# Streaming-encoder block: waits per half, spare banks in the mixer, one u tile ahead of the last scores, and index steps of four heads for the dense blocks

## The reference, cut to what matters

```python
hn = rmsnorm(x, mix_norm_w)                       # x: 512 tokens x 1024
z, xbc, dt, q, k, v = split(hn @ w_in)
y_ssd  = rmsnorm_per_group(ssd(silu(conv(xbc)), dt) * silu(z))    # Mamba-2, 8 heads, chunks of 64, state carried on
y_diff = rmsnorm_per_head(softmax(q1 k1) v - lam * softmax(q2 k2) v)   # 4 heads, chunk-causal
x = x + concat(y_ssd, y_diff) @ w_out
xb = rmsnorm(x, ffn_norm_w)                       # PEER, for every token:
sc = (xb @ w_q) . sub_keys                        # 8 heads x 2 halves x 128 keys
s, i = top_k(sc, 16)                              # per half
top_s, pos = top_k(s[0] + s[1], 16)               # of 16 x 16 candidates
idx = (i[0] * 128 + i[1])[pos];  g = softmax(top_s)
h = gelu(u[idx] @ xb)                             # u, v: 16384 x 1024
out = x + sum((g * h) * v[idx])                   # 128 experts for each token
```

## Time and profile before

| what | value |
|---|---|
| median of three runs | 1458.4 us (1455.88 to 1465.24) |
| the profiled execution | 1465.86 us, span 1464.1 us |
| TensorE busy | 1384.9 us, 95% of the span |
| VectorE busy | 1124.6 us, 77% |
| ScalarE busy | 392.5 us, 27% |
| GpSimd busy | 621.6 us, 42% |
| moved | 466.65 MB, mean 319 GB/s |

### The profile page before, as it was taken

The page is one execution under the profiler, slowest core; times in us unless marked ns, Lnnn a source line. Parts: engine busy times, 40 slices in busy tenths (PEclk is TensorE's granted clock), DMA queues, the critical chain, the costliest instruction groups (busy, mean ns, idle before and its releaser), DMA issues.

```text
span 1464.1 us, 16370 instructions
## 1 busy us (share of the span) xinstructions
PE 1384.9 (95%) x5430; PEld 941.3 (64%) x5430; DVE 1124.6 (77%) x2672; ACT 392.5 (27%) x1073; POOL 621.6 (42%) x516
## 2 busy tenths in 40 slices
PE   7999999997989999999999989999999999999994
PEld 5656647555478888878899879985444444444441
DVE  3445445699889999989999889997777767775667
ACT  3323332334221112012377667672000000000000
POOL 0000000331735542342466656666376755654541
PEclk9999999999999999999999999999999999999997
DMA  6423334773999998798799999999999999999997
GB/s 215 149 90 121 115 136 159 274 280 130 383 364 377 373 331 295 251 381 288 245 387 392 368 366 377 382 380 376 400 374 409 409 410 409 409 410 409 409 409 309
DMA packets 140084, 466.65 MB, mean 319 GB/s; under 512 B 14560, under 2 KB 14944, under 8 KB 139232
## 3 DMA queue, kind: packets, MB, share of 16 engines
q0 software_dynamic: 73728, 268.47, 47.8%
q1 hardware_dynamic: 66272, 197.14, 35.8%
HBM read 461.36 MB, written 4.19 MB: 318 GB/s over the span
## 4 chain that ended last, share of the span: by engine, by line
DVE 33%; DMA 28%; PE 24%; issue 9%; POOL 5%; ACT 1%; SPq 0%; another core or an unknown queue 0%; DVEq 0%; ACTq 0%; POOLq 0%
PE BANKS L597 10%; DMA UV<-v,IDX 9%; DVE X L1371 8%; DMA BIG<-v,IDX 7%; DMA BIG<-u,IDX 6%; PE BANKS L591 6%; DMA UV<-u,IDX 5%; PE BANKS L811 4%; POOL UV L1416 4%; DVE UV L1366 2%; DVE BIG L1366 2%; POOL BIG L1416 2%; DVE BIG L1205 2%; DVE BIG L1197 2%; DVE BIG L1199 1%
## 5 line engine op out<-in xcount | busy, mean ns | idle before, releaser
L1416 POOL DMA_INDIRECT UV<-u,IDX x154 | 186.7, 1212 | 385.7 <-DVE IDX L1256 262.8
L1416 POOL DMA_INDIRECT UV<-v,IDX x156 | 198.6, 1273 | 179.9 <-DVE UV L1366 107.1
L786 PE MATMUL BANKS<-T 128*128 128x256 f32 x1024 | 233.1, 383 | 3.5 <-issue 2.7
L1371 DVE SCALAR_TENSOR_TENSOR X<-UV,HG,X 128x1024 f32<-128x1024 f32 x156 | 200.3, 1284 | 44.8 <-DMA UV<-v,IDX 40.6
L786 PE MATMUL BANKS<-T,Y 128*128 128x256 f32 x1024 | 229.7, 380 | 0.1
L811 PE MATMUL BANKS<-T,BIG 128*128 128x512 f32 x512 | 225.4, 593 | 1.5 <-DVE BIG L1387 1.5
L811 PE MATMUL BANKS<-Y,BIG 128*128 128x512 f32 x512 | 225.1, 592 | 0.0
L1366 DVE SCALAR_TENSOR_TENSOR UV<-UV,Y 128x1024 f32<-128x1024 f32 x154 | 187.0, 1223 | 42.7 <-DMA UV<-u,IDX 41.0
L786 PEld LDWEIGHTS BANKS<-T 128*128 128x128 f32 x1024 | 193.7, 192 | 30.7 <-issue 4.5
L786 PEld LDWEIGHTS BANKS<-T,Y 128*128 128x128 f32 x1024 | 192.6, 191 | 25.5 <-DMA Y<-u_t 0.5
L1416 POOL DMA_INDIRECT BIG<-u,IDX x102 | 120.3, 1180 | 154.6 <-DVE X L1371 50.6
(11 more groups left out here) (255 smaller groups left out, 1204.4 us busy)
## 6 DMA issues: line engine op xcount, KB each, us to landing
T<-u_t SPq DMA_DIRECT2D x64, 512.0 KB
Y<-u_t SPq DMA_DIRECT2D x64, 512.0 KB
T<-v SPq DMA_DIRECT2D x64, 512.0 KB
Y<-v SPq DMA_DIRECT2D x64, 512.0 KB
BIG<-w_in SPq DMA_DIRECT2D x24, 1024.0 KB, 7.3
BIG<-w_q SPq DMA_DIRECT2D x16, 1024.0 KB, 7.9
BIG<-w_out SPq DMA_DIRECT2D x8, 1024.0 KB, 6.1
UV<-v,IDX POOLq DMA_INDIRECT x156
```

The source lines that it names most:

```text
L786: last = nc.tensor.matmul(PS[i % 4][:, 0:HT], ub[:, c, :], T8[:, 1, c, :], start=(c == 0), stop=(c == KC - 1))
L1371: stt(xb, row, HG[:, n % 2, i % UNIT:i % UNIT + 1], xb, ALU.mult, ALU.add).then_inc(used, 1)
L1416: pool.indirect_dma_start(row_place(s), None, u if kind == "ru" else v, bass.IndirectOffsetOnAxis(IDX[:, b, c:c + 1], 0)).then_inc(row_in[ ...
```

## The change

1. **Segment sums:** the second group of `S1` goes to bank 3, so TensorE no longer waits for VectorE between the groups (`seg_ready` wait removed).
2. **SSD ends:** for the last block the decayed copy and the state update are left out, since nothing reads them; for the first block the state is a copy, in place of a multiplication and an addition to zeros.
3. **Join, per half:** in `n2` the SSD half of the norm is done by ScalarE (`n_half`) in place of VectorE; half of each `T` is copied out by ScalarE (`t_late`) in four 128-wide pieces; three transposes take banks 4 to 7 (`T_BANK`); w_out and w_q products wait for the half of their operand that they need; the norm of `F` signals at its half (`f_half`); a K step waits head by head.
4. **Order of the join:** see the listings behind the diff; five more rows stand ahead of `S2(2)`; x tile 15 and W tile 15 stand ahead of the values of their steps.
5. **First u tile:** `gl 0` stands ahead of K 14 and K 15. u tiles 2 and 3 are loaded into X, and the first gelus use bank (i + 2) % 4.
6. **Dense keys:** the eight index steps of two heads become four of four heads (n = 9, 11, 13, 15), with masks in KT3; `sel 0` on ScalarE waits for all four (`dense_keys`); the first two one-hots come before the last keys of the sparse blocks.
7. **Planner:** new costs, and a limit of 3.44 us for each u tile. Ahead of u tile 0 now stand 82 rows (77 before), ahead of u tile 64 158 (153), ahead of the last `gm` 302 (297).
8. **Smaller ones:** three quarters of the set-aside scores go to HBM and back in place of all; row places in XBC and K open earlier.

```diff
@@ line 134 @@
-            out += then[:1] + on("C", i) if ended else on("C", i)
+            ahead = ended or i % 8 == 6
+            out += then[:1] + on("C", i) if ahead else on("C", i)
...
@@ line 137 @@
-            out += then[1:] if ended else then
+            out += then[1:] if ahead else then
...
@@ line 142 @@
-    after[7] += on("N n2", 1) + on("R0", 0) + on("T", 1) + many("cv", 8, 10) + on("R0", 1) + many("cv", 10, 12) + on("R1 Q", 0)
-    after[7] += many("cv", 12, 14) + on("F", 0) + on("R1 Q", 1) + on("U", 0) + on("F", 1) + on("k", 2) + on("k", 3) + on("U", 1)
+    after[7] += on("N n2", 1) + on("R0", 0) + on("T", 1) + many("cv", 8, 10) + on("R1 Q", 0) + many("cv", 10, 12)
+    after[7] += on("R0", 1) + many("cv", 12, 14) + on("F", 0) + on("R1 Q", 1) + on("U", 0) + on("F", 1) + on("k", 2)
+    after[7] += on("U", 1) + on("k", 3)
...
@@ line 151 @@
-    o += pick(0) + on("z", 2) + on("k2", 1) + on("S1", 2) + on("z", 3) + many("qt", 4, 6) + rows(4)
+    o += pick(0) + on("z", 2) + on("k2", 1) + on("S1", 2) + on("z", 3) + many("qt", 4, 6) + rows(9)
...
@@ line 163 @@
-    after[15] += rows(2) + on("F", 2) + rows(3) + on("R1 Q", 3) + on("U", 2) + many("K", 4, 6) + on("F", 3) + many("K", 6, 8) + on("U", 3) + rows(7)
+    after[15] += rows(4) + on("F", 2) + rows(1) + on("R1 Q", 3) + on("U", 2) + many("K", 4, 6) + on("F", 3) + many("K", 6, 8) + on("U", 3) + rows(7)
...
@@ line 166 @@
-    o += rows(12) + many("W", 24, 28) + many("K", 12, 14) + pick(3) + rows(9) + many("W", 28, 32) + many("K", 14, 16)
+    o += rows(12) + many("W", 24, 28) + many("K", 12, 14) + pick(3) + rows(9) + many("W", 28, 32) + on("gl", 0) + many("K", 14, 16)
...
@@ line 168 @@
-    cost = {"r": 6.2, "y": 5.0, "ru": 1.31, "rv": 1.29, "e": 0.0, "hg": 0.0, "H": 0.2, "w": 0.6, "ws": 1.0, "sel": 0.0, "oh": 1.0}
+    cost = {"r": 4.9, "y": 8.6, "ru": 1.22, "rv": 1.25, "e": 0.0, "hg": 0.0, "H": 0.2, "w": 0.6, "ws": 1.0, "sel": 0.0, "oh": 1.0}
...
@@ line 170 @@
-    for n in (8, 9, 10, 11, 12, 13, 14, 15, 4):
-        first, second, keys = pick(n)
-        work += [first] + rows(3) + (on("oh", 0) if n == 4 else []) + [second] + rows(3) + [keys] + rows(2 + n % 2)
+    for n in (9, 11, 13, 15):
+        for q, item in enumerate(many("r", 4 * (n // 2), 4 * (n // 2) + 4)):
+            work += [item] + rows(4 - (n >= 13))
+            if (n, q) == (13, 1):
+                work += on("ws", 2)
+        work += on("y", n) + rows(3)
...
@@ line 175 @@
-        if n in (12, 4):
-            work += on("ws", 2 + (n == 4))
-        if n == 14:
-            work += on("sel", 0)
+    first, second, keys = pick(4)
+    work += [first] + rows(2) + on("sel", 0) + rows(2) + on("oh", 0) + [second] + rows(3) + on("oh", 1) + [keys]
+    work += rows(1) + on("ws", 3)
...
@@ line 181 @@
-        o += on("gl", j)
-        while w < len(work) and spent < 4.1 * (j + 1):
+        o += on("gl", j) if j else []
+        while w < len(work) and spent < 3.44 * (j + 1) - 4:
...
@@ line 189 @@
-        if g + 1 < NGRP:
+        if 0 < g < NGRP - 1:
...
@@ line 454 @@
+        def turned(b):
+            return (t_done, 2 * NB + TURNS[("T", b)] + 1), (t_late, TURNS[("T", b)] + 1)
...
@@ line 512 @@
-                if j == 2:
-                    sp.wait_ge(ks_full, 16)
+                if j in (2, 3):
+                    sp.wait_ge(x_away, 16)
+                if j in (6, 7):
+                    sp.wait_ge(ks_full, 12 if j == 6 else 16)
...
@@ line 520 @@
-                    sp.wait_ge(hd_full, NKEY - NS + j + 1)
+                    sp.wait_ge(hd_full, NKEY - (NKEY - 1 - j) % NS)
...
@@ line 525 @@
-                        sp.dma_start(SC_BACK.rearrange("p a n -> p (a n)"), away).then_inc(sc_back, 16)
+                        sp.dma_start(SC_BACK[:, 1:4, :].rearrange("p a n -> p (a n)"), away).then_inc(sc_back, 16)
...
@@ line 552 @@
+                    if kind and c == 0:
+                        pe.wait_ge((n_half, f_half)[kind - 1], b + 1)
+                    else:
+                        pe.wait_ge(y_ready, y_count(kind, b))
...
@@ line 589 @@
+                    if halves and c % 4 == 0:
+                        pe.wait_ge(*halves[c // 4])
...
@@ line 594 @@
-            def tokens(b, n, bank, signal):
+            def tokens(b, n, bank, signal, halves=()):
...
@@ line 625 @@
-                    if g:
-                        pe.wait_ge(seg_ready, b * NG + g)
...
@@ line 628 @@
-                        last = nc.tensor.matmul(PS[2][:, h * P:(h + 1) * P], DAB[:, g * HPG + h, :], TRI,
+                        last = nc.tensor.matmul(PS[2 + g][:, h * P:(h + 1) * P], DAB[:, g * HPG + h, :], TRI,
...
@@ line 648 @@
+                if b == NB - 1:
+                    return
...
@@ line 754 @@
-                    pe.wait_ge(t_done, t_count(1, i) + 2)
-                    tokens(i, wo_at[c0], bank_01(RES[(step, i)] % 2, res_free, RES[(step, i)] + 1), res_full)
+                    tokens(i, wo_at[c0], bank_01(RES[(step, i)] % 2, res_free, RES[(step, i)] + 1), res_full,
+                           turned(i))
...
@@ line 762 @@
-                    channels(half, j, n, bank_01(j % 2, q2_done, i + 1), q2_full)
+                    channels(half, j, n, bank_01(j % 2, q2_done, i + 1), q2_full,
+                             [(ut_done, 4 * half + 3 + c) for c in range(2)])
...
@@ line 769 @@
+                        pe.wait_ge(q2_done, 2 * PH * half + hj + 1)
...
@@ line 776 @@
-                        pe.wait_ge(ks_done, 16)
...
@@ line 778 @@
+                    if i == 2:
+                        pe.wait_ge(ks_done, 16)
...
@@ line 784 @@
-                    ub = STREAM[i % NS].rearrange("p (c i) -> p c i", i=NKEY)
+                    ub = u_place(i).rearrange("p (c i) -> p c i", i=NKEY)
...
@@ line 947 @@
+                elif step == "n2":
+                    act.wait_ge(yrs_done, ROOTS[("N", i)] + 1)
+                    for g in range(NG):
+                        y = Y[:, i, g * 256:(g + 1) * 256]
+                        last = nc.scalar.activation(y, y, ACT.Copy, scale=NSQ[:, i, g:g + 1])
+                    last.then_inc(n_half, 1)
+                elif step == "T":
+                    act.wait_ge(t_full, t_count(1, i) + 2)
+                    for k in range(4):
+                        last = nc.scalar.activation(T8[:, i // 2, 4 + k, i % 2 * P:(i % 2 + 1) * P],
+                                                    PS[T_BANK(1, i) + 1][:, k * P:(k + 1) * P], ACT.Copy,
+                                                    scale=WC[:, 4 + k:5 + k])
+                    last.then_inc(t_late, 1)
...
@@ line 982 @@
-                    n, bank = KW[i], PS[i % 4]
+                    n, bank = KW[i], PS[(i + 2) % 4]
...
@@ line 1002 @@
+                    act.wait_ge(dense_keys, len(DENSE))
...
@@ line 1153 @@
-                        last = ts(SEG[:, g, h * P:(h + 1) * P], PS[2][:, h * P:(h + 1) * P],
+                        last = ts(SEG[:, g, h * P:(h + 1) * P], PS[2 + g][:, h * P:(h + 1) * P],
...
@@ line 1162 @@
-                dve.wait_ge(dt_act, 6)
-                tt(hd3(XDTE), hd3(XDT), bc(DTE[:, b, :], 2, HD), ALU.mult).then_inc(xdt_ready, 1)
+                if b < NB - 1:
+                    dve.wait_ge(dt_act, 6)
+                    tt(hd3(XDTE), hd3(XDT), bc(DTE[:, b, :], 2, HD), ALU.mult).then_inc(xdt_ready, 1)
...
@@ line 1184 @@
-                dve.wait_ge(st_full, b + 1)
-                link(tt(hd3(ST), hd3(ST), bc(CD[:, b, :], 2, HD), ALU.mult))
-                tt(ST, ST, PS[1][:, :], ALU.add).then_inc(st_ready, 1)
-                dve.wait_ge(st_ready, b + 1)
+                if b < NB - 1:
+                    dve.wait_ge(st_full, b + 1)
+                    if b == 0:
+                        nc.vector.tensor_copy(ST, PS[1][:, :]).then_inc(st_ready, 1)
+                    else:
+                        link(tt(hd3(ST), hd3(ST), bc(CD[:, b, :], 2, HD), ALU.mult))
+                        tt(ST, ST, PS[1][:, :], ALU.add).then_inc(st_ready, 1)
+                    dve.wait_ge(st_ready, b + 1)
...
@@ line 1254 @@
-                link(nc.vector.reduce_sum(isel[:, 1, :], oh, AXX))
-                if b < HB:
+                last = nc.vector.reduce_sum(isel[:, 1, :], oh, AXX)
+                if b >= HB:
+                    last.then_inc(dense_keys, 1)
+                    dve.wait_ge(dense_keys, DENSE[("y", n)] + 1)
+                else:
+                    link(last)
...
@@ line 1332 @@
-                    y3 = Y[:, i, 0:SSDW].rearrange("p (g d) -> p g d", g=NG)
-                    tt(y3, y3, bc(NSQ[:, i, 0:NG], 2, 256), ALU.mult)
...
@@ line 1350 @@
-                    stt(Y[:, i, :], X[:, i, :], SS[:, i:i + 1], FW, ALU.mult, ALU.mult).then_inc(y_ready, 1)
+                    for c, signal in enumerate((f_half, y_ready)):
+                        part = slice(c * HALF, (c + 1) * HALF)
+                        stt(Y[:, i, part], X[:, i, part], SS[:, i:i + 1], FW[:, part], ALU.mult, ALU.mult)\
```

(1 more changed line is left out.)

100 lines of the change are left out of this document (56 added, 44 removed).

## The result

The changed kernel takes 1435.7 us (median of four runs, 1434.52 to 1437.76), the kernel before 1457.71 in the same comparison. The ratio is 0.984, with a 95% interval of 0.980 to 0.988: 1.6% faster. The forecast was 1433, its range 1420 to 1449. Beside later experiments the kernel before took 1461 to 1466 us, so kernels that did not run beside each other are compared by their ratios to it, or by times inside their traces.

A forecast was written before the change was run, and what follows sets the result against it. Bound: when TensorE reaches the v tiles and how many rows are left then. Mixer 19.8, clock 1, dense half 0.3 and v stage 4 sum to 25.1 us off the 1458.4 median: 1433 us, range 1420 to 1449.

The forecast's parts named there:

- Term 1: Mixer segment sums: TensorE's waits for VectorE between the two groups go, 5.3 us; nothing is late next.
- Terms 2, 3 and the clock: First-half join: net 2.0 us; U 1 ahead of the last k product: 0.8; fewer gaps spare slow clock: 1.
- Term 4: Scores: K pairs wait less for ScalarE's fourth copy; 0.33 us at four places, 1.3 in all, none before z 2.
- Term 5: Second attention half: VectorE's own chain counts; fewer waits and operations there and one covered wait give 5.3 us.
- Terms 6 to 8: Second-half join 1.5 us; U 2 and U 3 chain 2.4; K 14 and K 15 behind u tile 0, 1.2.
- rival A: Rows are the pace, transfers nearly full from 371 us on; 10 to 15 us stay, 1443 to 1449; chance 0.15.
- The table load: Mixer's end: the 1.28 us load before the second root goes; at the skill's 2.66 the time would be 1432.
- Dense half: 481 to 710 us: four-head steps save VectorE 11, but TensorE waits about 4; gain 0.3, range 0 to 3.
- The stall: At 622 to 626 us, 7 us on TensorE: the change does not touch it; it need not be in every run.
- v stage: Five rows fewer save 6.4 to 7 us, unit 5's gathers cost 3, fewer set-aside scores give 0.6; net 4.
- C: Slower: ScalarE's sel 0 waits for all four dense steps, gelus queue behind it; 1465 to 1480 us; chance 0.05.
- B: No net change beyond 8 us, the waits only change places; 1450 to 1458 us; chance 0.08.

The follow-up runs named there:

- experiment 5: Changed kernel with both groups of the segment sums in bank 2 again and TensorE's wait between them; 1443.42 us, ratio 0.985 to the kernel before.
- second profile: Changed kernel run and profiled once more with no edit; 1436.38 us, ratio 0.982 to the kernel before.
- experiment 6: Changed kernel with both halves of each T copied out by VectorE, none by ScalarE; 1440.27 us, ratio 0.984 to the kernel before.
- experiment 3: Changed kernel with four rows ahead of S2(2), not nine; 1441.92 us, ratio 0.985 to the kernel before.
- experiment 7: Changed kernel with u tile 0 behind K 14 and K 15 again; 1444.44 us, ratio 0.983 to the kernel before.
- experiment 2: Kernel before without two row places in V's part of BIG; 1460.74 us against 1460.98, ratio 1.000.
- experiment 10: Changed kernel with sel 0 three u tiles earlier; 1434.37 us, ratio 0.981 to the kernel before.
- experiment 12: Changed kernel with sel 0 three u tiles earlier and four more rows, two of them behind the keys; 1427.65 us, ratio 0.977 to the kernel before.
- experiment 11: Changed kernel with four more rows between sel 0 and the first one-hot; 1429.06 us, ratio 0.978 to the kernel before.

## Why the prediction was right

The time, the sign and the way were right, 1433 for 1435.7. How near it came is in part luck. In the profiles the mixer gained 17.5 us for 20.8, the stretch from the second u tile to the first v tile 6.6 for 0.3 and the end 6.6 for 4, together 30.7 for 25.1; the medians, against which the sum was set, are 22.0 apart, and the interval of the ratio leaves 18 to 29.

- **Term 1, segment sums: right in kind, a little less in size.** 5.3 forecast. Undoing it costs 5.3 at the second u tile beside the first profile, but that match is luck: that profile has a slow tile, and the run of experiment 5 has a slow stretch of its own. Up to R0 of block 2, beside the second profile and without the clock, it costs 4.6. "Nothing is late next" was not quite so: in place of 1.59 and 1.22 TensorE now waits 0.42 and 0.56 for VectorE's copy ahead of the sums (250.84, 279.55).
- **Terms 2, 3 and the clock: right in size.** The join took 4.9 us less (from 167.45 to 217.65, then 165.38 to 210.72) for 2.0 + 0.8 and 1.7 of clock. The 0.6 charged for ScalarE's copies was right where it was placed (0.66 at 155.85); without them the first half is 0.7 us faster, and what they give in the second is not settled (experiment 6).
- **Term 4: mis-sized.** 1.3 was forecast for four places, one of them in the first half, and nothing ahead of z 2. The first half alone gained 1.3 (32.9 us from the w_q tile to the product behind the scores, then 31.6), 0.7 at each of its two places, that ahead of z 2 included; the waits of 0.47 are gone entirely.
- **Term 5, second attention half: the step that failed in the mixer.** From the first product after the scores to R0 of block 2 the gain is 3.5 us, 5.2 in the second profile, which has no slow tile. Terms 1 and 5 had 8.1 for it. By the second profile attention itself gained 2.4 (from 60.1 us to 57.7) for 2.0 forecast, but the SSD ahead of it 2.8 (60.1 to 57.3) for 6.1. Those 6.1 were the segment sums, 2.8 on TensorE and again 1.2 on VectorE, and three operations of VectorE, 2.1. "Its own chain counts" is what was wrong: VectorE is busy 56 of 59 us in attention, but only 46 of the 61 ahead of it, and there TensorE's own course sets the time. What it gained is 1.8 in its waits for the segment sums and 0.9 for the state product of the last block (L652 at 308.04), which the change leaves out and no term had. The segment sums were so counted twice. The cover of 7.48 us was used up by gathers that came 2.84 us late, which the prediction named as what would make it wrong; with five rows less the gain is 0.85 more (R0 of block 2 at 356.09 in experiment 3, 356.94 in the second profile).
- **Terms 6 to 8: right** up to the w_q tile (3.6 of 3.9). Behind it 1.7 us of clock came back, and 2.7 went to waits at the keys and at 448 that no term had, both for transfers that landed just then. This is the mechanism of rival A in small: where everything is sooner, the transfers are not. The 0.47 and 0.69 of term 8 are gone, but not by its order (experiment 7).
- **The table load:** The earlier trace rows and the changed kernel agree. The first root's load at 383.35 takes 1.28 us and stands ahead of the wait for the root's input, which ends at 387.95, so it costs nothing there. The Trainium skill (ScalarE: Activation LUTs, What ACT_TABLE_LOAD costs) gives about 2.66 us for a switch; none of these rows shows more than 1.3.
- **Dense half: mis-sized.** 0.3 us forecast, with 0 to 3 as range. Undoing the four-head keys costs 3.5 to 4.8 us in the trace and 3.3 in the time. The mechanism was right, VectorE waiting for `sel 0` and TensorE then 4 us for a one-hot (5.05 and 3.63). What failed is the state it was compared with: the 2.93 us of the earlier trace rows looked like all that TensorE waited for VectorE, but the stall of 7 us stood ahead of it, and without the stall that wait is 7.74. The change has 3.63 in place of 7.74.
- **The stall: wrong.** "The change does not touch it" fell: both profiles of before have it, neither of the changed kernel does, and it goes with the burst of gathers ahead of it (experiment 2). In the profiles this is most of the 6.6 us that the dense half gained. That it need not be in the sum held, since removing it alone gave 0.0% (-0.2 to 0.2), but the prediction's reason, that it need not be in every run, is not what the runs show: the wait behind it grew in its place.
- **v stage: right in kind.** Five rows left at TensorE's end (four to eight forecast), 6.6 us gained for 4. That is what the five rows alone were to give (6.4 to 7); the 3 us charged for the gathers of unit 5 do not show at the end, though the first of them waited 12.76 us (10.26).
- **The signs named:** u tile 0 at 461.89 is just outside 456 to 461, the first v tile at 977.92 inside 976 to 984, the largest one-hot wait under 5.
- **Rivals.** C did not come: no gelu held TensorE up. B neither. A fits experiment 10, where TensorE's 3.6 us came back as small waits while VectorE waited more for rows, but not all of experiment 12, where the order of VectorE's work brought the wait back. Four rows moved are worth 5 us at the end (experiment 11).

## What to carry to other kernels

A wait that the profile shows is what is left after the waits ahead of it: before you price a gap, ask what the same engine would wait for if an earlier stall were not there. A gap that two engines share counts once, and what a step on one engine saves counts on another only where that other waits for it: ask for each stretch anew which engine sets its pace. A wait that two causes can end, here a late transfer and a late copy at 448 us, does not go when one of them goes. Two profiles of one kernel can differ by 2 us in the mixer, as much as some of the effects looked for: compare an experiment with both. And where a stream of transfers fills the rest of the program, an idle stretch of the engine that consumes the stream can be filled with its items; here that gave 5 us at the end for four rows.

## What the runs showed of the hardware

- Three engines stood still together (TensorE 0.3 to 1.0 us at a time, VectorE 1.1 to 2.6, ScalarE up to 13.5 with little to do) at the end of 13 to 19 gathers issued without a pause, at 622 to 629 us in both profiles of the kernel before and at 601 to 603 with five rows less; with 11 in a row, and once with 13, TensorE had no such gap, nor with up to 20 in the v stage. Taking two row places away removed burst and stall. The Trainium skill (Trainium Architecture — The Big Picture, What this means for kernel authors) names a port that VectorE and GpSimd share as the only one that contends among the engines; a stall that stops TensorE and ScalarE as well is more than that rule covers. What the engines lack in it is open.
- The same tile of 16 records took 3.72 us in one execution and 5.41 in another, behind a gap of 0.95 and of 1.53 us, and 3.72 behind 1.82 in experiment 6, so the last gap alone does not decide; 64 records took 14.05 or 16.79, behind 1.42 and 3.13 us. Early in the v stage 8 records took 3.70 us behind gaps of 0.99 to 1.94, 5.40 behind 1.97 and 2.56, and 6.71 behind 3.61. The granted clock was 0.72 in the 6 us of the tile of 5.41, 0.72 in the 6 us around the first of those of 5.40, and 0.58 in the 8 us of that of 6.71.
- A table load on ScalarE took 1.28 us and ran ahead of the wait of the activation behind it (383.35, activation at 387.95).
